# The first layer's in-projection from high and low parts of its operands, with the residual kept in DRAM meanwhile

## The chip, the cores and the metric

The kernel runs on one core of one Trainium2 chip. The metric is the device time of one execution, in microseconds (us), as the median over runs. A core has a matrix engine (TensorE, PE in the rows), a vector engine (VectorE, DVE), a scalar engine (ScalarE, ACT), a general engine (GpSimd, POOL) and SyncE (SP), whose queue issues the weight transfers here. The engines run side by side and meet at semaphores.

## The reference, cut to what matters

Two layers act on 256 context tokens and 256 latent tokens of width 1024. Of the first layer only the input projection is touched:

```python
u_l = rmsnorm(h_l, norm_g[l, 0]) * (1 + sc_a) + sh_a
u_c = rmsnorm(h_c, norm_g[l, 0]) * (1 + csc_a) + csh_a
...
def mixer_ab(u_c, u_l, w_in, w_out, ...):
    p_c = split_cols(u_c @ w_in, AB_SPLITS)
    p_l = split_cols(u_l @ w_in, AB_SPLITS)
    ...
    (q, k, v, output gate | input and forget gates | z, x with B and C, dt)
...
h_l = h_l + g_a * rmsnorm(y_l, norm_g[l, 1])
```

`u` is 512 tokens by 1024, `w_in` is 1024 by 5424 columns: q and k 512 each, v and the output gate o 1024 each, 16 gate columns, z 1024, x (with B and C) 1280, dt 32. After it come an mLSTM and an SSD scan, an output projection, a residual and a mixture of experts; the second layer is of the same size.

## The kernel before, in words

Activations lie transposed in SBUF: feature on the 128 partitions, 512 tokens along the row, so `u` is eight tiles `a_u[:, k, :]` (k = 0 to 7). The residual `h` has the same shape and stays in SBUF for the whole program. The program is a sequence of blocks with a barrier of all engines between them. Weights stream through a ring of three slots of 2 MB (`ring`, pieces of 1024 rows by 512 columns); SP issues piece i once piece i-3 was let go, in a fixed order.

The in-projection is two blocks. `project_gates` makes three small outputs (`pg` 0 to 2: 8, 8 and 32 rows) and then ten tiles of 128 columns of x by 512 tokens. `project_rest` makes 32 such tiles in the order q, k, v (two halves), o (two), z (two), four to a piece. Every tile is eight float32 matmuls (one for each k) into one PSUM bank (`mms`, L358); the trace holds two records for one float32 matmul. The tiles of v have `u` as the stationary operand, all others the weights. Behind each group of four tiles PE also sums one piece of the modulation weights (`row_sums`, L468), and turns a row of those sums (`turn_row`, L475).

In `project_rest` ACT first takes its part in two softplus-like functions (`soft_act`, L713 and L715: an Exp and a Ln, each of which waits for DVE), once for the forget gates and once for dt, and then evicts each tile from PSUM (`pr`, five banks in turn). DVE works out the gate rows (`mlstm_rows`, `ssd_rows`) and then the convolution of ten tiles of x: five operations each (L781 once, L783 four times), with a Silu on ACT (L863) behind each. From the third tile on DVE waits for the Silu of two tiles before. PE needs the rows of DVE once, in `turn_rows`. POOL has nothing to do in this block.

A scheme of high and low parts is already used in two later stages of this kernel, `out_projection` of layer 0 (L1202 to L1214) and `project_rwkv` of layer 1 (L1894 to L1914). There ACT copies an operand into a tile of type float32r (the high part), POOL subtracts that from the weights (the low part, 128x1024 at a time), DVE subtracts it from the activations, and PE adds three products:

```python
def three(wh, wl, xh, xl):
    return [(wh, xh), (wh, xl), (wl, xh)]
```

So a tile of 128x512 over k = 0 to 7 is 24 matmuls of float32r there, one record each, instead of 8 of float32.

## Time and profile before

| | |
|---|---|
| runs | 2682.89, 2684.81, 2694.09 us, median 2684.81 us |
| the profiled execution | 2680.09 us, with a span of 2678.3 us between its first and last instruction |
| granted TensorE clock, mean | 0.895 of full speed |
| PE busy | 2189.2 us, 82% of the span |
| weight loads of PE | 1353.1 us, 51% |
| DVE busy | 988.4 us, 37% |
| ACT busy | 650.2 us, 24% |
| POOL busy | 248.0 us, 9% |

The page also cuts the span into 40 slices of 67 us and gives each engine's busy share in tenths. The two blocks of the in-projection run from 76.7 to 416.3 us, which is the second to the seventh digit. Matmuls are pipelined and their ends are modelled, so starts are the firmer numbers. A number in brackets behind a row is how long the engine had been idle, and for whom.

### The profile page before, as it was taken

The numbers are of one execution on the slowest core, as the hardware profiler recorded it, in microseconds if no ns is written. First come the engines' busy times: TensorE is split into PE (matmuls) and PEld (weight loads), VectorE is DVE, ScalarE is ACT, GpSimd is POOL, SyncE is SP. The second block draws the span as 40 slices with busy tenths as digits, with TensorE's granted clock in tenths as the row PEclk, the third lists the DMA queues.
The fourth block names the chain that finished last, engine by engine and source line by source line (L and its number), as shares of the span: only waits on it lengthen the run. The fifth ranks groups of instructions, "written<-read, shape, count | busy, mean of one in ns | idle before, by whom it ended". The sixth has DMA issues, their size and how long they took to land. (4 is left out here: it accounts for less than half of the span.)

```text
span 2678.3 us, 56972 instructions
## 1 busy us (share of the span) xinstructions
PE 2189.2 (82%) x25395; PEld 1353.1 (51%) x25395; DVE 988.4 (37%) x1594; ACT 650.2 (24%) x1441; POOL 248.0 (9%) x190
## 2 busy tenths in 40 slices
PE   4899999789888897798837869868888889777766
PEld 2344444433375544454423348657887766634333
DVE  0243204666622311111142347556677652311112
ACT  2011213335532200010021232354553420100001
POOL 0000000000043100000010015313131100100000
PEclk8999998888898798899978989979999988797888
DMA  6244431050134459887843013000000023499994
GB/s 212 71 168 153 150 126 63 1 189 0 35 123 160 148 205 326 317 274 263 290 169 111 0 37 105 0 2 4 4 4 4 4 73 118 162 373 349 348 325 159
DMA packets 180666, 376.76 MB, mean 141 GB/s; under 512 B 11210, under 2 KB 40486, under 8 KB 180422
## 3 DMA queue, kind: packets, MB, share of 16 engines
q1 hardware_dynamic: 162830, 339.82, 35.7%
q10 hardware_dynamic: 14136, 20.72, 2.5%
q0 software_dynamic: 3456, 12.58, 1.3%
q8 instruction: 200, 3.28, 0.5%
q14 instruction: 44, 0.36, 0.0%
HBM read 632.36 MB, written 23.86 MB: 245 GB/s over the span
## 5 line engine op out<-in xcount | busy, mean ns | idle before, releaser
L358 PE MATMUL banks<-arena,ring 128*128 128x512 f32 (+3 forms) x1136 | 420.1, 531 | 25.9 <-PEq L305 25.9
L358 PEld LDWEIGHTS banks<-arena,ring 128*128 128x128 f32 (+2 forms) x1136 | 212.3, 188 | 227.9 <-issue 217.0
L1453 PE MATMUL banks<-arena 128*32 128x256 f32 x1696 | 238.0, 430 | 97.4 <-DMA arena<-in_exp_w_up_dram 97.3
L1454 PE MATMUL banks<-arena 128*32 128x256 f32 x1696 | 238.0, 430 | 0.0
L358 PE MATMUL banks<-parts 128*128 128x512 f32 (+1 forms) x1032 | 216.2, 372 | 23.7 <-DVE parts L372 20.5
L358 PEld LDWEIGHTS banks<-parts 128*128 128x128 f32 x1032 | 182.4, 192 | 57.2 <-DVE parts L372 11.5
L1453 PEld LDWEIGHTS banks<-arena 128*32 128x32 f32 x1696 | 107.0, 121 | 189.1 <-DMA arena<-in_exp_w_up_dram 106.1
L2109 PE MATMUL banks<-arena 64*64 64x64 f32 x4224 | 159.9, 225 | 49.2 <-DVE arena L369 18.9
L366 DVE TENSOR_TENSOR arena<-banks,arena 64x256 f32<-64x256 f32 (+3 forms) x128 | 65.2, 511 | 319.2 <-ACT arena L1517 250.2
L2109 PEld LDWEIGHTS banks<-arena 64*64 64x64 f32 x4224 | 148.1, 140 | 53.4 <-DVE arena L369 20.4
L1517 ACT ACTIVATE arena<-banks 64x256 f32<-64x256 f32 x78 | 29.7, 381 | 584.5 <-PE banks L1454 584.5
L2109 PE MATMUL banks<-ring 64*64 64x64 f32 x4224 | 158.7, 224 | 7.2 <-issue 7.0
L358 PE MATMUL banks<-arena 128*64 128x128 f32 (+9 forms) x492 | 132.9, 423 | 36.8 <-PEq L305 25.0
L2109 PEld LDWEIGHTS banks<-ring 64*64 64x64 f32 x4224 | 146.6, 139 | 9.4 <-issue 8.7
L1475 PE MATMUL banks<-arena 128*32 128x256 f32 x1696 | 111.5, 407 | 17.3 <-DMA arena<-in_exp_w_down_dram 17.3
L358 PEld LDWEIGHTS banks<-arena 128*128 128x128 f32 (+5 forms) x492 | 73.3, 194 | 88.8 <-issue 60.0
L1453 PE MATMUL banks<-ring,arena 128*32 128x256 f32 x800 | 102.1, 399 | 8.1 <-DMA ring<-in_exp_w_up_dram 8.0
L1454 PEld LDWEIGHTS banks<-arena 128*32 128x32 f32 x1696 | 106.5, 121 | 0.0
L1214 POOL TENSOR_TENSOR parts<-ring,parts 128x1024 fp32r<-128x1024 f32 x16 | 38.5, 2410 | 711.0 <-ACT parts L1202 711.0
L1454 PE MATMUL banks<-ring,arena 128*32 128x256 f32 x800 | 101.9, 399 | 0.0
L1113 PE MATMUL banks<-arena 128*64 128x256 f32 (+3 forms) x288 | 89.3, 465 | 13.8 <-DVE arena L1146 13.8
L358 PE MATMUL banks<-ring,arena 128*128 128x512 f32 x224 | 98.4, 596 | 1.6 <-DVE arena L366 1.6
(321 smaller groups left out, 3123.2 us busy)
## 6 DMA issues: line engine op xcount, KB each, us to landing
arena<-in_exp_w_gate_dram SPq DMA_DIRECT2D x106, 1024.0 KB
arena<-in_exp_w_up_dram SPq DMA_DIRECT2D x106, 1024.0 KB
arena<-in_exp_w_down_dram SPq DMA_DIRECT2D x53, 2048.0 KB
ring<-in_exp_w_gate_dram SPq DMA_DIRECT2D x50, 1024.0 KB
ring<-in_exp_w_up_dram SPq DMA_DIRECT2D x50, 1024.0 KB
ring<-in_exp_w_down_dram SPq DMA_DIRECT2D x25, 2048.0 KB
ring<-in_w_mod_dram SPq DMA_DIRECT2D x24, 2048.0 KB, 8.3
ring<-in_ab_w_in_dram SPq DMA_DIRECT2D x10, 2048.0 KB, 11.4
```

Source lines behind the costliest of these rows:

```text
L358: m = nc.tensor.matmul(o, a, b, start=first and n == 0, stop=last and n == len(pairs) - 1)
L366: return nc.vector.tensor_tensor(o, a, b, ALU.mult)
L1113: m = nc.tensor.matmul(o[:, c0:c1], a_xt[:, s, hd * SSP:(hd + 1) * SSP], weights_of[it % 3][:, s, c0:c1], start=d == 0 and k == 0, stop=d ...
L1214: nc.gpsimd.tensor_tensor(w_low[:, t % 2], landed(t), whole(w_high[:, t % 2]), ALU.subtract).then_inc(pool_done, pool.tick(("w low", t), * ...
L1453: nc.tensor.matmul(o[r:r + BLOCK, 0:256], x, up[:, k, c], start=k == 0, stop=k == KD - 1)
L1454: m = nc.tensor.matmul(o[64 + r:64 + r + BLOCK, 0:256], x, gate[:, k, c], start=k == 0, stop=k == KD - 1)
L1475: m = nc.tensor.matmul(ps[3 + i % 2][BLOCK * q:BLOCK * q + BLOCK, 0:256], x, w[:, k, 256 * q:256 * q + 256], start=k == 0, stop=k == 3)
L1517: nc.scalar.activation(m_sil[0:64, :], ps[i % 2][64:P, 0:256], ACT.Silu).then_inc(act_done, act.tick(("silu", i)))
L2109: m = nc.tensor.matmul(view(d, n_)[half(d, hf, n_), p, :], now[d][a][rows, p, :], now[d][b][rows, p, :], start=q == 0, stop=q == len(pairs ...
```

## The change

The projection's inputs and weights are split into high and low parts, and each tile is three products over k instead of one. The three small outputs (`pg` 0 to 2) keep float32 operands, `a_u_plain`, which lies where `a_u` lay.

- `u`: ACT writes the high part `u_high` over the room of `h` (`h_parts`), DVE the low part `u_low` in place over `a_u_plain`, from `pg` 2 on, since the three small outputs read `a_u_plain`. For that `h` is stored to DRAM in the block ahead (`save_h`) and loaded again in the block `mlstm` behind.
- weights: for each of 42 jobs (ten in `project_gates`, 32 in `project_rest`) ACT writes a high part and POOL a low part (`split_high`, `split_low`), 128x1024 each, into two rooms in turn; job j may be split once PE is through with job j-2 ("used"). The rooms lie in the later place of z's output, and for the jobs of z in the convolution's room. A weight piece is let go by POOL's last subtraction, and no longer by PE.
- `project_gates` splits jobs 0 to 11, that is its own ten and the first two of the next block. In `project_rest` ACT splits two jobs ahead, in one stream with the evictions.
- v is taken by pieces of 256 rows: a job is two k by 512 columns, times four token tiles, and the four banks are evicted together after the fourth job.
- `row_sums` stands behind the second tile of each group instead of the fourth, `turn_rows` behind job 15 instead of 9, and the Silus of the convolution behind jobs 12 to 21 instead of 8 to 17. `out_projection` and all that follows is as before.

```diff
--- before.py
+++ after.py
-        h = sb("h", [P, KD, T])
+        with nc.sbuf_tensor("h", [P, KD, T], F32) as h:
+            pass
+
+        h_parts = ctx.enter_context(nc.sbuf_tensor("h_parts", [P, KD, T], F32R))
...
+        h_saved = nc.dram_tensor("h_saved", (P, KD, T), F32, kind="Internal").ap()
+        h_saved_done = semaphore("h_saved_done")
...
+        with nc.sbuf_tensor("arena_ahead_of_u", [P, 22608], F32), nc.sbuf_tensor("a_u_plain", [P, KD, T], F32) as a_u_plain:
+            pass
+
+        ctx.enter_context(nc.sbuf_tensor("arena_for_experts", [P, 5120], F32))
+        parts_z = ctx.enter_context(nc.sbuf_tensor("parts_z", [P, 4096], F32R))
+        ctx.enter_context(nc.sbuf_tensor("arena_between", [P, PARTS - 9216], F32))
...
+        split_jobs = [(("x", 2), f) for f in range(2)] + [(key, f) for key in (
+            ("x", 0), ("x", 1), "q", "k", ("v", 0), ("v", 1), ("o", 0), ("o", 1), ("z", 0), ("z", 1)) for f in range(4)]
+        rooms_of_parts = split_rooms()
...
+        def split_high(j):
+
+            i = piece_at[split_jobs[j][0]]
+            act.wait_ge(weights_landed[i % NSLOT], 16 * (i // NSLOT + 1))
+            act.wait_ge(*at(("used", j - 2)))
+            nc.scalar.activation(parts_of(j)[0], landed_part(j), ACT.Copy).then_inc(act_done, act.tick(("w high", j)))
+
+        def split_low(j, *also):
+
+            high, low = parts_of(j)
+            key, f = split_jobs[j]
+            pool.wait_ge(*at(("w high", j)))
+            for label in also:
+                pool.wait_ge(*at(label))
+            last = f == (1 if key == ("x", 2) else 3)
+            nc.gpsimd.tensor_tensor(low, landed_part(j), whole(high), ALU.subtract).then_inc(
+                pool_done, pool.tick(("w low", j), *((let_go(key),) if last else ())))
+
+        N_GATE_JOBS = 10
+        u_low = parts_region(22608 - PARTS, KD, T)
...
+                for j in range(N_GATE_JOBS):
+                    o = bank("pg", 3 + j)
+                    high, low = parts_of(j)
+                    if j == 0:
+                        pe.wait_ge(*at(("u high", KD - 1)))
+                        pe.wait_ge(*at(("w high", 0)))
+                        mms(o, [(high[:, k, :], u_high[:, k, :]) for k in range(KD)], last=False)
+                        pe.wait_ge(*at(("w low", 0)))
+                        mms(o, [(low[:, k, :], u_high[:, k, :]) for k in range(KD)], first=False, last=False)
+                        for k in range(KD):
+                            pe.wait_ge(*at(("u low", k)))
+                            m = mms(o, [(high[:, k, :], u_low[:, k, :])], first=False, last=k == KD - 1)
+                    else:
+                        pe.wait_ge(*at(("w low", j)))
+                        pairs = []
+                        for k in range(KD):
+                            pairs += three(high[:, k, :], low[:, k, :], u_high[:, k, :], u_low[:, k, :])
+                        m = mms(o, pairs)
+                    m.then_inc(pe_done, pe.tick(("pg", 3 + j), ("used", j)))
+
+            def act_():
+                split_high(0)
+                split_high(1)
+                act.wait_ge(h_saved_done, 16)
+                for k in range(KD):
+                    nc.scalar.activation(u_high[:, k, :], a_u_plain[:, k, :], ACT.Copy).then_inc(act_done, act.tick(("u high", k)))
+                for j in range(2, N_GATE_JOBS + 2):
+                    split_high(j)
...
+                    if j == 3:
+                        for k in range(KD):
+                            dve.wait_ge(*at(("u high", k)))
+                            vsub(u_low[:, k, :], a_u_plain[:, k, :], whole(u_high[:, k, :])).then_inc(dve_done, dve.tick(("u low", k)))
...
+                for j in range(N_GATE_JOBS + 2):
+                    split_low(j, *([("pg", 2)] if j == 1 else []))
...
-                    w = weights(key)
-                    if j >= 5:
-                        pe.wait_ge(*at(("pr", "read", j - 5)))
-                    c = slice(f * P, (f + 1) * P)
-                    pairs = [(a_u[:, k, c], w[:, k, :]) if key[0] == "v" else (w[:, k, c], a_u[:, k, :]) for k in range(8)]
-                    mms(ps[j % 5], pairs).then_inc(pe_done, pe.tick(("pr", j), *((let_go(key),) if f == 3 else ())))
-                    if j == 9:
+                    J = N_GATE_JOBS + j
+                    high, low = parts_of(J)
+                    pe.wait_ge(*at(("w low", J)))
+                    if key[0] == "v":
+                        for tt in range(TT):
+                            t = j - f + tt
+                            if f == 0:
+                                pe.wait_ge(*at(("pr", "read", t - 5)))
+                            c, pairs = slice(tt * P, tt * P + P), []
+                            for k in range(2):
+                                pairs += three(u_high[:, 2 * f + k, c], u_low[:, 2 * f + k, c], high[:, k, :], low[:, k, :])
+                            m = mms(ps[t % 5], pairs, f == 0, f == 3)
+                            if f == 3:
+                                m.then_inc(pe_done, pe.tick(("pr", t), *((("used", J),) if tt == TT - 1 else ())))
+                        if f < 3:
+                            m.then_inc(pe_done, pe.tick(("used", J)))
+                    else:
+                        if j >= 5:
+                            pe.wait_ge(*at(("pr", "read", j - 5)))
+                        pairs = []
+                        for k in range(KD):
+                            pairs += three(high[:, k, :], low[:, k, :], u_high[:, k, :], u_low[:, k, :])
+                        mms(ps[j % 5], pairs).then_inc(pe_done, pe.tick(("pr", j), ("used", J)))
+                    if j == 15:
                         turn_rows()
                     m = 4 + j // 4
                     if f == 0 and m > 4:
                         turn_row(0, m - 1, scratch[:], ps[6])
-                    if f == 3:
+                    if f == 1:
...
+                for j, (key, f) in enumerate(jobs):
+                    if j == 22:
+                        act.wait_ge(*at(("conv silu", 9)))
+                    if j + 2 < len(jobs):
+                        split_high(N_GATE_JOBS + j + 2)
+                    if key[0] != "v":
+                        evict(j, key, f)
+                    elif f == 3:
+                        for tt in range(TT):
+                            evict(j - 3 + tt, key, tt)
...
-                    if 8 <= j < 18:
-                        t = j - 8
+                    if 12 <= j < 22:
+                        t = j - 12
...
+            def sp_():
+                sp.wait_ge(h_saved_done, 16)
+                load(nc.sync, h[:], h_saved)
...
+        def save_h():
+
+            nc.sync.dma_start(h_saved, h[:]).then_inc(h_saved_done, 16)
...
-        modulated("u", 0, 0, a_u, 26704)
+        modulated("u", 0, 0, a_u_plain, 26704, sp_=save_h)
```

The order of instructions moves at two places. The first is PE's stream in `project_gates`. Before, behind the three small outputs (8 and 32 rows) the tiles of x follow; `arena` is `a_u`, `ring` the weights:

```order
L358 MATMUL banks<-arena,ring 8x512 [waits weights_landed_1]
L358 MATMUL banks<-arena,ring 8x512 x15
L358 MATMUL banks<-arena,ring 32x512 [waits weights_landed_2]
L358 MATMUL banks<-arena,ring 32x512 x7
L358 MATMUL banks<-arena,ring 128x512 x16
```

Of the change; `h_parts` is `u_high`, `parts_z` holds the weights' two parts, `parts` is `u_low`:

```order
L368 MATMUL banks<-a_u_plain,ring 32x512 [waits weights_landed_2]
L368 MATMUL banks<-a_u_plain,ring 32x512 x7
L368 MATMUL banks<-h_parts,parts_z 128x512 [waits scalar_steps_done]
L368 MATMUL banks<-h_parts,parts_z 128x512 x7
L368 MATMUL banks<-h_parts,parts_z 128x512 [waits gpsimd_steps_done]
L368 MATMUL banks<-h_parts,parts_z 128x512 x7
L368 MATMUL banks<-parts,parts_z 128x512 [waits vector_steps_done] x8
```

The first tile of x now has 24 matmuls in three groups, of which the last eight each wait for DVE's subtraction of one k.

The second place is ACT's stream from the start of `project_rest`. Before, with the second Exp and Ln of `soft_act` ahead of the evictions of q (L847):

```order
L713 ACTIVATE arena<-arena 32x512 [waits vector_steps_done]
L715 ACT_TABLE_LOAD
L715 ACTIVATE arena<-arena 32x512 [waits vector_steps_done]
L847 ACTIVATE arena<-banks 128x512 [waits tensor_steps_done] x4
L480 ACTIVATE scratch<-banks 128x512 [waits tensor_steps_done]
```

Of the change (L793 and L795 are the Exp and the Ln, L680 is `split_high`, L944 the eviction of q, L490 the copy of a modulation row):

```order
L793 ACTIVATE arena<-arena 32x512 [waits vector_steps_done]
L795 ACT_TABLE_LOAD
L795 ACTIVATE arena<-arena 32x512 [waits vector_steps_done]
L680 ACTIVATE parts_z<-ring 128x1024 [waits tensor_steps_done]
L944 ACTIVATE arena<-banks 128x512
L680 ACTIVATE parts_z<-ring 128x1024 [waits tensor_steps_done]
L944 ACTIVATE arena<-banks 128x512
L490 ACTIVATE scratch<-banks 128x512 [waits tensor_steps_done]
```

The splitting for the third tile of q (the first L680 here) stands behind the last Ln on the same engine.

## Rows read from the trace of the kernel before

**Rows 1.** The page, the span in 40 slices: busy tenths of PE and DMA, granted clock
```profile
PE   4899999789888897798837869868888889777766
PEclk8999998888898798899978989979999988797888
DMA  6244431050134459887843013000000023499994
```
**Rows 2.** The timeline of PE from 50 to 440 us: start, duration, instruction
```profile
76.67 91.24 PE L358 MATMUL banks<-arena,ring 128*8 128x512 f32 x208 [11.62 <-PEq L305]
169.50 27.70 PE L358 MATMUL banks<-arena,ring 128*128 128x512 f32 x64 [1.60 <-PEq L305]
197.13 1.92 PE L468 MATMUL banks<-ring,silc 128*32 128x512 f32 x16
...
227.55 1.92 PE L468 MATMUL banks<-ring,silc 128*32 128x512 f32 x16
...
416.29 1.09 PE L919 MATMUL banks<-arena,ident 8*128 8x512 f32 x2 [1.03 <-PEq L305]
```
**Rows 3.** The timeline of DVE from 140 us, and of all engines at 99 us
```profile
99.08 0.68 DVE L665 COPY arena<-banks 32x512 f32<-32x512 f32 x1 [6.19 <-PE banks L358]
...
161.07 0.69 DVE L668 COPY arena<-banks 128x512 f32<-128x512 f32 x1 [6.17 <-PE banks L358]
167.94 0.69 DVE L668 COPY arena<-banks 128x512 f32<-128x512 f32 x1 [6.18 <-PE banks L358]
```
**Rows 4.** The timeline of ACT in out_projection, 740 to 830 us
```profile
739.44 8.41 ACT L1207 ACTIVATE parts<-arena 128x512 fp32r<-128x512 f32 x16
752.97 1.06 ACT L1202 ACTIVATE parts<-ring 128x1024 fp32r<-128x1024 f32 x1 [5.12 <-PE banks L358]
...
823.69 1.06 ACT L1202 ACTIVATE parts<-ring 128x1024 fp32r<-128x1024 f32 x1 [4.38 <-PE banks L358]
```
**Rows 5.** The tile parts: duration ns min/median/max, first and last start
```profile
L1894 POOL TENSOR_TENSOR parts<-ring,parts x27: 2343/2395/2795, 1582.0 to 1714.7; 128x1024 fp32r<-128x1024 f32 x27
L372 DVE TENSOR_TENSOR parts<-arena,parts x24: 676/677/2834, 740.1 to 1590.6; 128x512 fp32r<-128x512 f32 x24
```
**Rows 6.** The timeline of PE in out_projection
```profile
745.66 88.87 PE L358 MATMUL banks<-parts 128*128 128x512 f32 x384 [9.19 <-DVE parts L372]
```
**Rows 7.** The timeline of ACT from 140 us: start of project_rest
```profile
169.47 1.28 ACT L713 ACT_TABLE_LOAD   x1 [93.16 <-PEq L305]
...
193.48 0.63 ACT L715 ACTIVATE arena<-arena 32x512 f32<-32x512 f32 x1
```
**Rows 8.** The timeline of DVE: first tile of the convolution
```profile
204.26 0.55 DVE L781 TENSOR_SCALAR arena<-arena,vec 128x512 f32<-128x512 f32 x1
204.84 3.11 DVE L783 SCALAR_TENSOR_TENSOR arena<-arena,vec 128x512 f32<-128x512 f32 x4
```
**Rows 9.** The timeline of all engines in project_rwkv
```profile
1627.71 2.40 POOL L1894 TENSOR_TENSOR parts<-ring,parts 128x1024 fp32r<-128x1024 f32 x1 [3.97 <-ACT parts L1902]
1628.22 2.44 DVE L369 TENSOR_TENSOR arena<-arena 128x512 f32<-128x512 f32 x1 [2.75 <-ACT arena L1914]
```
**Rows 10.** The timeline of ACT: eviction of o and a Silu
```profile
298.94 0.60 ACT L853 ACTIVATE arena<-banks 128x512 f32<-128x512 f32 x1 [4.62 <-PE banks L358]
299.56 1.28 ACT L863 ACT_TABLE_LOAD   x1
300.85 0.63 ACT L863 ACTIVATE arena<-arena 128x512 f32<-128x512 f32 x1
```
**Rows 11.** The DMA issues: line, count, KB, median us to landing
```profile
ring<-in_w_mod_dram SPq DMA_DIRECT2D x24, 2048.0 KB, 8.3
ring<-in_ab_w_in_dram SPq DMA_DIRECT2D x10, 2048.0 KB, 11.4
```
**Rows 12.** Two stretches: busy us (count) PE, PEld, DVE, ACT, POOL; clock, DMA share, GB/s
```profile
60.00:70.00 10.00, 5.05 (x11) 1.49 (x10) 4.06 (x3) 4.86 (x8) 0.00 (x0) 0.99 0.00 0
...
736.00:760.00 24.00, 14.81 (x59) 12.16 (x59) 13.47 (x19) 12.44 (x20) 7.93 (x4) 0.73 0.55 175
```

## What the change should do to the time, foretold before it was run

> **What bounds the kernel now.** I read the page first. PE is near 9 tenths in the second to the seventh slice and its clock there is near full [rows 1]; these slices are the in-projection. The timeline of PE says how tightly: records of the projection follow each other from 76.67 us, with one gap of 1.6 us at 169.5, up to the first instruction of the next block at 416.29 [rows 2]. Nobody is waited for inside, so this stretch is as long as PE's own work, and a shorter tile shortens the program one for one, as long as whoever feeds PE keeps up. DVE's evictions in project_gates give the period of a float32 tile: 167.94 - 161.07 = 6.87 us [rows 3]. The rest block lasts 416.29 - 169.50 = 246.8 us; 32 tiles are 219.8 of it, and 27.0 are all else: eight row sums of 1.9 us [rows 2], the turned rows, the hand-over.
>
> **What a tile costs in three products.** The same form is in the trace: out_projection makes 24 products of 128x512 per weight room, and ACT begins its next split when PE is through with a room. From 752.97 to 823.69 there are 13 such periods, 70.72 / 13 = 5.44 us [rows 4], that is 0.227 us a product. 42 tiles would save 42 x (6.87 - 5.44) = 60.1 us if PE never waited. The feeders per job are one ACT copy, 1.06 us [rows 4], and one POOL subtraction, 2.4 us, at most 2.8 [rows 5]. From the end of tile j to the low part of tile j+2 that is about 3.7 us with a tenth for each of two semaphores, and tile j+1 covers 5.44. In steady state they are hidden with 1.7 us to spare; without that cover each pair of tiles would lose what the chain has over 5.44.
>
> What is left is where the cover is missing.
>
> **project_gates.** The three small outputs stay; `pg` 2 is evicted at 99.08 [rows 3]. By then ACT has made the first two weight parts and u_high (eight copies at 8.41 / 16 = 0.53 us each [rows 4]), from 76.7 to about 83. The store of h is issued when the block ahead starts, before 60 us; no transfer ran from 60 to 70 us there [rows 12], and a weight piece of 2 MB lands in 8.3 to 11.4 us [rows 11], so it has landed by 75, against a need at 79. I cost it at nothing; the cover is the small outputs, and it costs only if it lands after 95. PE can do 16 of the first 24 products at once (3.6 us, to 102.7). The last eight wait for DVE's subtractions, which DVE begins behind the eviction, at 99.8. POOL's subtraction of job 1 is released by the same `pg` 2 and starts first. Beside such an operation a DVE addition took 2.44 us, started at 1628.22 and over 0.55 us after POOL's end [rows 9], and the longest u-type subtraction took 2.83, where the median is 0.68 [rows 5]. So the first of the eight ends near 102.2 and the last near 107.1; tile 0 ends at 107.4, 2.9 us late. (Without the collision it would be 105.5.) Nine more tiles: 107.4 + 49.0 = 156.4.
>
> **The hand-over.** Job 11 is split in this block and may only start when tile 9 is done: 0.1 + 1.06 + 0.1 + 2.4, and POOL must end before the barrier. Then the barrier as before, from DVE's end at 167.94 + 0.69 = 168.63 to 169.50 [rows 2, 3], 0.9. PE starts the next block at 161.0 and not at 158: 3.0 us more of gap than before.
>
> **project_rest, its start.** This is the largest loss. Jobs 10 and 11 are ready, and job 12 is split by ACT behind the second Ln. In the trace of before ACT ends that Ln at 194.11, in a block that began for it at 169.47: 24.6 us [rows 7], most of it waiting for DVE's gate rows. Before this cost nothing, since PE had tiles that needed only a free bank. Now job 12 is ready at 24.6 + 1.1 + 0.1 + 2.4 + 0.1 = 28.3 us, while PE has work for 2 x 5.44 + 1.9 (row sums) = 12.8. PE stands for 15.5 us. POOL has nothing to do until then, so DVE's rows take no longer. Behind a wait PE comes back at a lower clock: out_projection began at 745.66 after 9.19 us idle [rows 6], was through with its first room at 752.97, 7.3 us and not 5.44, and the stretch shows 0.73 of the full clock [rows 12]. That is 1.9 us once; the same loss at the hand-over, if it comes, ends within the stall.
>
> **project_rest, the remainder.** 30 tiles are 163.2 us. Of the 27.0 us of other work 1.9 lie ahead of the stall, and about 0.7 at the end fall away, since the last row sums now have two tiles behind them: 24.4. The four evictions of v (0.6 each behind a split of 1.06) make the next token tile wait once, 0.5. End: 28.3 + 163.2 + 24.4 + 1.9 + 0.5 = 218.3 us after 161.0, that is 379.3 against 416.3.
>
> **The sum**: 60.1 saved, 23.1 given back, **37.0 us** less. Everything behind is as before; reloading h, 2 MB, lies in `mlstm`, in whose two slices, the seventh and eighth, the DMA engines are busy for 1 tenth and none [rows 1]; I cost it at nothing, and it would cost only if that block were shorter than the 11 us of a landing [rows 11]. The profiled execution took 2680.1, so 2643.1; it lies 4.7 below the median of the runs (2684.8), from which the same saving gives 2647.8. I take 2646. What a measurement of this kernel can tell from no change is about 0.5%, 13.4 us.
>
> **The convolution** has to be weighed too. DVE's five operations on a tile take 0.55 + 3.11 and with gaps 3.7 us [rows 8]; each reads SBUF, and POOL now holds it off for 2.4 us in each tile's period. A period is 5.44 and with its share of row sums 6.2 us, which leaves 3.8. It just fits, with almost two periods between the release of a convolution and the Silu that needs it. If nothing collided it would cost 0; if every tile met POOL twice, 3.7 + 2 x 2.4 = 8.5 us against 6.2, over eight tiles 18 us, of which the slack takes some 5. I take 0 and keep 13 for the range. The Trainium skill ("SBUF — State Buffer", Who interferes with whom) says that a VectorE instruction with two SBUF inputs and a GpSimd one that reads SBUF exclude each other for the whole instruction. The trace agrees (2.44 us against 0.68), and by that rule the convolution is no freer than I put it.
>
> **ACT's tables.** Behind tiles 16 to 21 the Sigmoid of o and the Silu of the convolution alternate, so each needs two table loads, where before two tiles had that. The trace has an eviction at 298.94, the load at 299.56 for 1.28 us, and the Silu at 300.85 right behind it [rows 10]. ACT's work in such a period is 1.06 + 0.60 + 0.63 + 2 x 1.28 = 4.9 us, under 5.44. "ScalarE: Activation LUTs" (the Trainium skill, What ACT_TABLE_LOAD costs) adds a drain, and puts a switch at 2.66 us; the trace shows no such gap, and with that figure the period would be an estimated 7.6 us and the result that of the second rival below.
>
> **The rivals.**
> - Convolution late, as above: DVE paces tiles 14 to 21, saving near 24, **2657 to 2660**. For it: DVE has 0.1 us of spare in a period. Against it: the two periods of slack. 12 in 100.
> - ACT paces the tiles of o. If each switch held ACT for twice the row's 1.28 us, six periods would be 7.4 us each, 2.0 over 5.44, less the spare of 1.7 and the row sums: about 7 us, **2653**. Against it: the row. 3 in 100.
> - Weights late. The piece for the next group is let go about 3.7 us behind a group's second tile and is needed five tiles later, 21 us, two pieces at once. At 8.3 to 11.4 us each [rows 11] they fit even one behind the other; 5 us late in a few groups gives **2656**. 4 in 100.
> - The stall is shorter than I think, because something lets job 12 go early: **2630**. Nothing in ACT's order speaks for it. 3 in 100.
> - Slower: the chain from the end of a tile to the low part of the next but one is longer than a tile. Then the period is (chain + 5.44) / 2. The 37 us are gone when it is 1.23 us longer over 30 tiles, that is with a chain of 7.9 us instead of 3.7, and by 8.8 us the kernel is slower by 0.5%, **2698** and up. POOL's subtraction would have to take 7 us beside DVE's work; in 27 executions beside DVE none passed 2.8 [rows 5]. 2 in 100.
> - The change doesn't do what it says: products on these operands run no faster than those of float32, 6.87 a tile, and only the losses stay, 2680 + 23 = **2703**. The period of out_projection [rows 4] is against it. 1 in 100.
>
> My forecast, a saving of 30 to 43, has the remaining 75. The range of 8 in 10 goes from 2632 (a stall some 10 us shorter) to 2661 (the late convolution). Faster by over 0.5% (below 2671): 0.94. Within: 0.03. Slower: 0.03.
>
> **What would show it.** In the timeline of PE: tiles of 24 records 5.44 us apart; a wait for `parts` of DVE in the first tile of x; a gap near 5 us before the rest block; a gap of 15 us behind two tiles and one row sum, released by POOL's L690, whose own wait is for ACT L680; clock below 1.0 in the two stretches behind the gaps; the next block's first matmul near 379. Wrong would be a gap before each tile released by POOL (the chain), by ACT behind L971 (convolution or tables), or by a transfer (weights). Nothing past 379 should be shorter or longer by more than a few us.

## The result, and the profile after

The changed kernel takes 2657.46 us (median of 4 runs, 2651.06 to 2659.08) where the one before takes 2687.21 beside it: a ratio of 0.9891 (95% interval 0.9859 to 0.9922). A second set of 6 runs of it gave 2650.86 us (2646.89 to 2656.08) against 2686.93: 0.9868 [0.9837, 0.9899]. Both medians lie in the predicted range of 2632 to 2661, 11 and 5 us above the predicted 2646. As a saving that is 29.8 us in the first set, at the lower edge of the 30 to 43 that were forecast, and 36.1 in the second. The profiled execution took 2651.06 us with a span of 2649.3, where the sum had given 2643.1.

The page, the same three rows as in [rows 1] (PE's busy tenths, the granted clock, DMA):

```profile
PE   5879999788796987797838869867887888877776
PEclk7989998778897999998968889979999988888788
DMA  7244540320324478987731012000000023599994
```

The timeline of PE, to be laid beside [rows 2]. Line numbers have moved: L368 here is L358 there, L478 is L468, L1031 is L919.

```profile
75.42 22.52 PE L368 MATMUL banks<-a_u_plain,ring 128*8 128x512 f32 x48 [11.61 <-PEq L315]
97.86 4.00 PE L368 MATMUL banks<-h_parts,parts_z 128*128 128x512 f32 x16
101.70 4.53 PE L368 MATMUL banks<-parts,parts_z 128*128 128x512 f32 x8
...
160.10 0.47 PE L368 MATMUL banks<-h_parts,parts_z 128*128 128x512 f32 x1 [3.95 <-PEq L315]
...
172.93 1.92 PE L478 MATMUL banks<-ring,silc 128*32 128x512 f32 x16
188.14 0.80 PE L368 MATMUL banks<-h_parts,parts_z 128*128 128x512 f32 x1 [13.29 <-POOL parts_z L690]
...
380.48 1.09 PE L1031 MATMUL banks<-arena,ident 8*128 8x512 f32 x2 [1.04 <-PEq L315]
```

PE, which had one gap of 1.60 us before, now has two large ones: 3.95 us at the hand-over and 13.29 us behind two tiles and a row sum. The projection lasts from 75.42 to 380.48, 305.06 us, where it was 416.29 - 76.67 = 339.62: 34.6 us less. The whole execution is 29.0 less (2680.09 - 2651.06). The remainder is elsewhere: the projection begins 1.25 us earlier, and what follows it is 6.8 us longer (2649.3 - 380.48 = 2268.8 against 2678.3 - 416.29 = 2262.0). The last experiments deal with that.

The stretches of the projection (busy us with counts of PE, PEld, DVE, ACT, POOL; then the granted clock, DMA share, GB/s):

```profile
75.42:160.10 84.68, 80.09 (x288) 49.66 (x289) 15.99 (x21) 16.77 (x21) 30.13 (x15) 0.98 0.36 123
...
160.10:188.10 28.00, 14.75 (x64) 10.46 (x64) 25.43 (x32) 12.39 (x16) 2.36 (x2) 0.76 0.42 173
188.10:196.00 7.90, 7.86 (x27) 6.37 (x28) 7.62 (x9) 0.35 (x1) 2.77 (x1) 0.78 0.50 164
196.00:280.00 84.00, 83.75 (x411) 64.25 (x410) 27.38 (x28) 26.01 (x36) 34.04 (x14) 1.00 0.51 185
280.00:380.48 100.48, 99.44 (x482) 76.54 (x481) 25.35 (x32) 48.20 (x56) 35.26 (x15) 1.00 0.46 164
```

The second row is the stall: PE is busy for 14.75 of 28.00 us, DVE for 25.43 of them, and the clock is at 0.76. The third is the restart: PE is busy throughout, at a granted clock of 0.78, so about 7.9 x 0.22 = 1.7 us are lost. From 196 on the clock is full and up to the barrier at the end PE is out of work for 0.25 us only, behind the first half of v. The splits of weights and what holds that of the third tile of the block (job 12), in the timelines of ACT and of POOL:

```profile
111.82 1.06 ACT L680 ACTIVATE parts_z<-ring 128x1024 fp32r<-128x1024 f32 x1 [4.43 <-PE banks L368]
...
156.19 1.06 ACT L680 ACTIVATE parts_z<-ring 128x1024 fp32r<-128x1024 f32 x1 [4.42 <-PE banks L368]
...
184.09 0.63 ACT L795 ACTIVATE arena<-arena 32x512 f32<-32x512 f32 x1
184.62 1.04 ACT L680 ACTIVATE parts_z<-ring 128x1024 fp32r<-128x1024 f32 x1
```
```profile
185.74 5.13 POOL L690 TENSOR_TENSOR parts_z<-ring,parts_z 128x1024 fp32r<-128x1024 f32 x2 [26.08 <-ACT parts_z L680]
```

The split (L680) of job 12 starts right behind the last Ln of the dt rows (L795), and POOL had stood for 26 us waiting for it. Ready at 188.14, that is 28.0 us into the block. Elsewhere splits follow PE's tiles: from 111.82 to 156.19 there are eight periods, 5.546 us each.

The changed kernel was profiled a second time, in the second set of runs (2651.25 us). A stretch of 305 us again and a median 28 to 30 us below the kernel before had been expected of it; the stretch took 307.17 us (the first block 86.03, the second 221.14), and the median is 36.1 us below. In the timeline of ACT the splits behind the first and the second tile of x:

```profile
109.37 1.06 ACT L680 ACTIVATE parts_z<-ring 128x1024 fp32r<-128x1024 f32 x1 [24.59 <-PE banks L368]
116.39 1.06 ACT L680 ACTIVATE parts_z<-ring 128x1024 fp32r<-128x1024 f32 x1 [5.96 <-PE banks L368]
```

The second tile took 7.0 us there and not 5.5. PE had waited for DVE in the last eight products of the tile ahead, and the granted clock from 109.08 to 116.30 was 0.76, where it was 1.00 over the same tile in the first profile. The restart behind the stall also cost more, 2.4 us. So the length of the stretch moves by 2 us between executions of the same kernel; of the six profiles that have this first tile with all its products and its waits, two show a second tile of 7 us.

### The profile page after: what moved, and what is told of

It reads as the page before. It is cut to its first block and busy times, and to the rows that moved or that the text cites. A ratio compares the mean times of both kernels' runs of the same rounds, so it can differ in the third digit from the quotient of the medians.

```text
span 2649.3 us, 57779 instructions
## 1 busy us (share of the span) xinstructions
PE 2141.1 (81%) x25731; PEld 1417.6 (54%) x25731; DVE 1010.6 (38%) x1602; ACT 706.4 (27%) x1499; POOL 350.6 (13%) x232
## 5 line engine op out<-in xcount | busy, mean ns | idle before, releaser
L368 PE MATMUL banks<-parts 128*128 128x512 f32 (+1 forms) x1096 | 241.0, 373 | 23.6 <-DVE parts L382 20.4
L368 PEld LDWEIGHTS banks<-parts 128*128 128x128 f32 x1096 | 194.3, 192 | 59.7 <-DVE parts L382 11.5
L368 PE MATMUL banks<-arena,ring 128*128 128x256 f32 (+2 forms) x544 | 161.7, 460 | 12.7 <-PEq L315 12.7
L368 PE MATMUL banks<-arena 128*64 128x128 f32 (+9 forms) x492 | 135.8, 430 | 36.8 <-PEq L315 25.0
L2225 PEld LDWEIGHTS banks<-ring 64*64 64x64 f32 x4224 | 143.3, 135 | 12.7 <-issue 12.2
L368 PE MATMUL banks<-h_parts,parts_z 128*128 128x512 f32 x416 | 133.9, 402 | 17.2 <-POOL parts_z L690 13.3
L368 PEld LDWEIGHTS banks<-arena,ring 128*128 128x128 f32 (+1 forms) x544 | 105.4, 195 | 67.1 <-issue 56.0
L368 PEld LDWEIGHTS banks<-arena 128*128 128x128 f32 (+5 forms) x492 | 74.3, 196 | 89.5 <-issue 60.5
L1784 POOL DMA_INDIRECT arena<-y_sorted,slot_ids x12 | 11.3, 945 | 746.1 <-DMA y_sorted<-arena 743.1
L1569 PE MATMUL banks<-ring,arena 128*32 128x256 f32 x800 | 99.9, 393 | 8.9 <-DMA ring<-in_exp_w_up_dram 8.9
L690 POOL TENSOR_TENSOR parts_z<-ring,parts_z 128x1024 fp32r<-128x1024 f32 x34 | 84.3, 2482 | 158.4 <-ACT parts_z L680 139.1
```

Of the source, the lines that this page charges most:

```text
L368: m = nc.tensor.matmul(o, a, b, start=first and n == 0, stop=last and n == len(pairs) - 1)
L690: nc.gpsimd.tensor_tensor(low, landed_part(j), whole(high), ALU.subtract).then_inc(pool_done, pool.tick(("w low", j), *((let_go(key),) if ...
L1569: nc.tensor.matmul(o[r:r + BLOCK, 0:256], x, up[:, k, c], start=k == 0, stop=k == KD - 1)
L1784: nc.gpsimd.indirect_dma_start(m_yg[:, t, a, :], None, y_sorted, bass.IndirectOffsetOnAxis(ap=slots[:, t, a:a + 1], axis=0)).then_inc(y_ga ...
L2225: m = nc.tensor.matmul(view(d, n_)[half(d, hf, n_), p, :], now[d][a][rows, p, :], now[d][b][rows, p, :], start=q == 0, stop=q == len(pairs ...
```

## The experiments

A single run is one execution: its total says little, and its profile is what is read. Three times named below are read off the timeline of PE in the same way everywhere: *gates* is project_gates, from its first matmul to the first of project_rest (84.68 us in the changed kernel), *rest* is from there to the first matmul of `mlstm` (220.38), and the stretch is their sum (305.06). Their counterparts before are 92.83, 246.79 and 339.62.

### The splits between the gate rows

The two exponentials of `em` and the dt rows are no longer ahead of the tiles in ACT's order: jobs 12 and 13 are split behind the first rows, job 14 behind `em`, the dt rows follow.

```diff
+                for j in range(2):
+                    one_job(j, *jobs[j])
                 for e in range(2):
...
+                one_job(2, *jobs[2])
                 soft_act(tmp32, "dt")
-                for j, (key, f) in enumerate(jobs):
+                for j in range(3, len(jobs)):
```

> ACT's stream at the start of project_rest is put in another order: splits and evictions of the first two tiles of q stand behind the first Ln, those of the third ahead of the second Exp. All work is done. Theory (the stall of 13 to 15 us behind two tiles comes from the place of the split in ACT's stream): the gap goes; the lower clock behind the hand-over, hidden until now, costs 1.9 us in its place, DVE's rows become a few us longer beside POOL, and the block of 220.4 us becomes 205 to 208. Rival (DVE's gate rows bind, wherever the splits stand): the gap only moves, and the block stays above 217. Against the kernel before: 40 to 45 us less in all, a ratio near 0.984.

Measured: 2642.44 us (4 runs), ratio 0.9833 [0.9817, 0.9849]. Rest 208.14 us, just over the 205 to 208 expected and 12.2 less than in the changed kernel, gates 84.55. PE's gap of 13.29 has become one of 2.42, behind another wait, in the timeline of ACT:

```profile
184.16 0.63 ACT L973 ACTIVATE arena<-arena 8x512 f32<-8x512 f32 x1 [7.72 <-DVE arena L841]
...
185.87 1.04 ACT L680 ACTIVATE parts_z<-ring 128x1024 fp32r<-128x1024 f32 x1
```

ACT waits 7.7 us for DVE's rows at `em`, and the split of the fifth tile of the block stands behind it. So the order on ACT was the cause of the stall: only the order was changed, and 11 of its 13 us went. DVE's rows themselves were slower here, because POOL works beside them now; in the timeline of DVE one addition takes 2.78 us

```profile
170.04 2.78 DVE L379 TENSOR_TENSOR arena<-arena 8x512 f32<-8x512 f32 x1
```

while POOL's subtraction runs from 169.55 to 172.28. In the changed kernel, where POOL stands idle, the same row takes 0.68 us.

### Saving and reloading h, alone

The kernel before, with nothing added but the two transfers of h.

```diff
+            def sp_():
+                sp.wait_ge(h_saved_done, 16)
+                load(nc.sync, h[:], h_saved)
...
-            block(pe_, act_, dve_)
+            block(pe_, act_, dve_, None, sp_)
...
-        modulated("u", 0, 0, a_u, 26704)
+        modulated("u", 0, 0, a_u, 26704, sp_=save_h)
```

> The kernel before with one part of the change alone: h is stored to DRAM in the block ahead of the projection and loaded again in mlstm; the projection stays in float32. Theory (it is hidden): the projection's 339.6 us and mlstm's 112.3 us stay within 1 us, ratio 1.000. Rival (the reload is what made mlstm 2.8 us longer after the change): mlstm has 115 us here too.

Measured: 2685.65 us (10 runs), ratio 0.9987 [0.9964, 1.0011]; gates 92.72, rest 246.79, stretch 339.51 against 339.62. The round trip costs nothing that can be measured, and the projection does not feel it. `mlstm`, with the reload in it, took 114.82 us, and not the 112.3 that were expected to stay within 1 us; that is the rival's 115, and the last experiment takes it up.

### Two products instead of three

One product in three is left out, that of the stationary operand's low part with the high part of the moving one: the weights' low part, and in the tiles of v that of `u`. So the projection is less exact than the reference asks for; the splitting, the waits and the transfers stay.

```diff
-                            pairs += three(high[:, k, :], low[:, k, :], u_high[:, k, :], u_low[:, k, :])
+                            pairs += three(high[:, k, :], low[:, k, :], u_high[:, k, :], u_low[:, k, :])[:2]
```

> The changed kernel with the third product of each k left out (low stationary part times high moving part) in the in-projection, so 16 products a tile and a less exact result; all splits are made as before. It asks how much of the chain ACT, POOL, DVE is covered. Theory: a tile is 3.7 us, about as long as the chain of 3.6 us; the ten tiles of project_gates take 3.7 to 3.8 us each; in project_rest the stall grows by 3.7 us to 17, and in the tiles of o, where ACT needs 4.9 us and DVE's convolution 6.1 beside POOL, the period is near 6 us and no longer 5.5. The stretch from the first matmul of project_gates to mlstm, 305.1 us, becomes 240 to 248. Rival (ACT alone sets the pace of o, DVE is not held off by POOL): 4.9 us in those tiles, 5 us less in all. Rival (feeders far from binding): 3.7 us throughout, the stretch 232.

Measured: 2592.36 us (4 runs), ratio 0.964 [0.9624, 0.9656]; stretch 241.87 (240 to 248 expected), gates 70.23. In the timeline of ACT the first two and the last of nine splits, then in that of PEld (weight loads) two waits:

```profile
112.65 1.06 ACT L680 ACTIVATE parts_z<-ring 128x1024 fp32r<-128x1024 f32 x1 [3.95 <-PE banks L368]
116.36 1.06 ACT L680 ACTIVATE parts_z<-ring 128x1024 fp32r<-128x1024 f32 x1 [2.64 <-PE banks L368]
...
143.14 1.06 ACT L680 ACTIVATE parts_z<-ring 128x1024 fp32r<-128x1024 f32 x1 [2.72 <-PE banks L368]
```
```profile
116.24 0.19 PEld L368 LDWEIGHTS banks<-h_parts,parts_z 128*128 128x128 f32 x1 [0.37 <-POOL parts_z L690]
119.95 0.19 PEld L368 LDWEIGHTS banks<-h_parts,parts_z 128*128 128x128 f32 x1 [0.18 <-POOL parts_z L690]
```

A tile is (143.14 - 112.65) / 8 = 3.81 us. Here the weight load of each tile waits 0.2 to 0.4 us for POOL: from the split at 116.36 to the weight load at 119.95 it is 3.6 us, with a semaphore ahead of it the 3.7 of the prediction. That chain is as long as a tile of 16 products, so it shows at last. Under tiles of 24 it is hidden with 1.8 us to spare, and there PE's own work, the products, sets the time of the changed kernel. The stall is 16.97 us, as expected.

The six tiles of o are another matter. Their period was expected near 6 us, or 4.9 if ACT alone set it:

```profile
265.32 0.64 ACT L970 ACTIVATE arena<-arena 128x512 f32<-128x512 f32 x1 [0.94 <-DVE arena L862]
265.86 1.04 ACT L680 ACTIVATE parts_z<-ring 128x1024 fp32r<-128x1024 f32 x1
```

From 249.61 to 277.42 there are five periods, 5.56 us each, with ACT never waiting for PE but once for 0.19, and for DVE's convolution (L862) up to 0.94. So where the tables alternate, ACT and DVE together need as long as a tile of 24 products: the changed kernel has next to nothing to spare there.

### The rooms of the parts elsewhere

Tiles took 5.49 to 5.55 us and not 5.44. The parts of the gates' jobs are put where those of z lie, and nothing else is changed.

```diff
-            high, low = rooms_of_parts[key[0] == "z"][j % 2]
+            high, low = rooms_of_parts[key[0] == "z" or j < 10][j % 2]
```

> The weight parts of the ten jobs of project_gates lie in the convolution's room (the one that z's jobs use) and not in z's output; nothing else. It tests why a tile takes 5.54 us in this block where out_projection has 5.44 and the jobs of z 5.48. Theory (it hangs on where the operands lie in SBUF): 5.48 here, the block 84.7 us becomes 84.1. Rival (it is DVE's evictions, transfers or the block's own waits): 5.54 stays.

Measured in a single run: 2648.96 us; gates 84.18, rest 220.60. Splits in the timeline of ACT:

```profile
112.60 1.06 ACT L680 ACTIVATE parts<-ring 128x1024 fp32r<-128x1024 f32 x1 [4.36 <-PE banks L368]
...
156.55 1.06 ACT L680 ACTIVATE parts_z<-ring 128x1024 fp32r<-128x1024 f32 x1 [4.38 <-PE banks L368]
```

The period is (156.55 - 112.60) / 8 = 5.494, where the same eight in the changed kernel give (156.19 - 111.82) / 8 = 5.546. The old place gives 5.546 to 5.548 in the three other profiles of the same eight periods (the first edit, the second profile of the changed kernel, the later reload), so the difference is no scatter: the place of the operands does set about 0.05 us of a tile, 2 ns a product. Gates became 0.5 us shorter. That is too little to be seen in the kernel's time, and what it is about the place is not shown.

### A gentler hand-over

From here on edits are added to the version with the splits between the rows. Job 11 is split at the start of project_rest instead of at the end of project_gates.

```diff
-                for j in range(2, N_GATE_JOBS + 2):
+                for j in range(2, N_GATE_JOBS + 1):
...
+                split_high(N_GATE_JOBS + 1)
```

> e1 with the split of job 11 moved over the barrier: ACT's and POOL's part for it are the first of project_rest. Theory: the gap of 3.95 us between the two blocks becomes 1.6 and the lower clock behind it goes, so project_gates is 2.3 us shorter; but DVE's rows now meet one more subtraction and begin half a us later, so ACT's exponentials and with them the split of job 14 come some 3 us later, and project_rest grows from 208.1 to 210 or 211: nothing gained in the sum. Rival (the rows have slack enough): project_rest stays at 208 or falls to 206, and the gain of 2.3 stays.

Measured in a single run: 2638.99 us; gates 82.35, rest 212.29, stretch 294.64 against 292.69 with the first edit alone: no net gain, as expected, but a loss of 2 us, since rest had been put at 210 to 211. In the timeline of PE:

```profile
161.86 0.47 PE L368 MATMUL banks<-h_parts,parts_z 128*128 128x512 f32 x1 [1.12 <-PEq L315]
...
192.61 0.79 PE L368 MATMUL banks<-h_parts,parts_z 128*128 128x512 f32 x1 [6.26 <-POOL parts_z L690]
```

The gap at the barrier falls from 3.95 to 1.12 (1.6 was expected): 2.8 us were the split of job 11. They come back at the next wait, 6.26 us where it was 2.42. That wait ends on DVE's rows, and these became later: POOL's subtraction of job 11 now runs beside the first of them, which takes 2.91 us (0.68 in the changed kernel), and ACT's exponentials of `em` start 25.4 us into the block instead of 23.1. The longer gap also brings the lower clock back: from 175 to 200 it is 0.86, where the first edit alone had 1.00.

### The low part early

POOL's subtraction of job 1 no longer waits for `pg` 2, so it does not start together with DVE's eight subtractions. A memset behind `pg` 2 lets the weight piece go in its place.

```diff
-            last = f == (1 if key == ("x", 2) else 3)
+            last = f == 3
...
-                    split_low(j, *([("pg", 2)] if j == 1 else []))
+                    split_low(j)
+                    if j == 1:
+                        pool.wait_ge(*at(("pg", 2)))
+                        nc.gpsimd.memset(slot_gate[:, 0:1], 0.0).then_inc(pool_done, pool.tick(let_go(("x", 2))))
```

> e5 with POOL's subtraction of job 1 freed from its wait for the third small output (a one-element memset behind that output lets the weight piece go instead), so that it runs at 80 us and no longer beside DVE's first subtraction of u. Theory (that collision cost 1.9 us): DVE's eight subtractions take 5.6 us and not 7.1, and the first tile of x ends 1.5 to 1.9 us sooner; project_rest as in e5. Rival (the eight are slow for another reason): no change.

Measured in a single run: 2637.55 us; gates 79.46, 2.9 less, rest 212.99 (212.29 before this edit). The collision in the changed kernel (all engines):

```profile
98.09 2.84 POOL L690 TENSOR_TENSOR parts_z<-ring,parts_z 128x1024 fp32r<-128x1024 f32 x1 [19.21 <-PE banks L368]
98.58 7.10 DVE L382 TENSOR_TENSOR parts<-a_u_plain,h_parts 128x512 fp32r<-128x512 f32 x8
...
102.12 0.19 PEld L368 LDWEIGHTS banks<-parts,parts_z 128*128 128x128 f32 x1 [0.41 <-DVE parts L382]
```

POOL runs from 98.09 to 100.93. DVE's eight subtractions, begun at 98.58, take 7.10 us; the later ones are 0.60 us each (0.19 of weight load and 0.41 of wait), so the first was through only 2.9 us after it began, and PE waits for each of the next. With the collision gone DVE's eight take 4.88 us, and the first tile's last eight products wait for nobody (the rows of the next experiment show the same). From its first product to the first of the second tile it is 6.00 us instead of 8.21, a gain of 2.2 where 1.5 to 1.9 had been expected. The other 0.7 us of the 2.9 are no gain: the small outputs ran at a lower clock in the profile of the version before (0.90 from 80 to 100 us, here 1.00).

### All together

Besides these, jobs 12 to 16 are split and the first five tiles evicted ahead of `em` and the dt rows, and the gates' parts lie in the room of z's.

```diff
-                for j in range(2):
+                for j in range(5):
                     one_job(j, *jobs[j])
```

> e6, the rooms of e4 for project_gates, and ACT's order changed further: the first five jobs of project_rest are split and evicted ahead of the exponentials of m and of the second soft_act, which wait for DVE. Theory (DVE's rows are not needed before the convolution, so nothing has to wait for them here): no gap behind the first tiles, project_gates 80 us and project_rest 203 to 205, the stretch 284 against 305.1 of the change and 339.6 before; about 2632 in the median, a ratio near 0.979. Rival (DVE's rows, now beside five subtractions, delay the convolution, and it paces the tiles of o): project_rest stays near 208, with ACT waiting for DVE behind tiles 14 to 21.

Measured: 2628.02 us (6 runs, 2622.03 to 2642.08), ratio 0.9794 [0.976, 0.9829]; gates 79.06, rest 203.88, stretch 282.94 (284 expected), which is 22 us less than in the changed kernel and 57 less than before. In the timeline of PE no gap over 0.25 us is left between the hand-over and the last turned row:

```profile
98.99 3.99 PE L368 MATMUL banks<-h_parts,parts 128*128 128x512 f32 x16
102.81 2.32 PE L368 MATMUL banks<-parts 128*128 128x512 f32 x8
104.97 0.39 PE L368 MATMUL banks<-h_parts,parts 128*128 128x512 f32 x1
...
357.61 0.95 PE L485 MATMUL banks<-quarter_sum,scratch 128*128 128x2 f32 x8
359.60 1.77 PE L1040 MATMUL banks<-arena,ident 8*128 8x512 f32 x2 [1.04 <-PEq L315]
```

Rest is 9.1 us less than in the version before: the gap of 6.3, and most of the remainder the restart behind it. All 6 runs are below all 6 of the changed kernel beside them (2646.89 to 2656.08), 22.8 us in the medians. With the losses taken away that the prediction had listed, 56.7 of the 60.1 us are had that it gave for the products alone.

### Is mlstm longer, and for the reload?

`mlstm` took 115.02 us after and 112.26 before, 2.8 of the 6.8 us that are lost behind the projection. It holds the reload of h. The kernel before with the round trip alone had 114.82, but one value of a block that may scatter decides nothing. Two versions reload `h` later, behind mlstm_out, and the kernel before ran twice more.

```diff
-            block(pe_, act_, dve_, None, sp_)
+            block(pe_, act_, dve_)
...
         def ssd_prepare():
...
-            block(pe_, act_, dve_)
+            def sp_():
+                sp.wait_ge(h_saved_done, 16)
+                load(nc.sync, h[:], h_saved)
+
+            block(pe_, act_, dve_, None, sp_)
```

> The kernel before once more, for the scatter of the blocks behind the in-projection. In its first profiled execution mlstm lasted 112.3 us (528.55 - 416.29); in the kernels that reload h inside mlstm it lasted 112.6 to 118.4, most about 115.5. Theory A, the reload lengthens mlstm by some 3 us: this run shows 112 to 113. Theory B, scatter between executions alone: this run may show anything from 112 to 118.

> The kernel before a third time. Theory A: mlstm 112 to 113 us again. Theory B: 112 to 118, so that its three values spread as those with the reload do.

> The changed kernel, but h is reloaded in the block behind mlstm_out (ssd_prepare) instead of in mlstm. Theory A (the reload of 2 MB costs mlstm some 3 us): mlstm 112 to 113 us, total about 2648 instead of 2651. Theory B (scatter): mlstm 112 to 118 and a total of 2647 to 2656, as the changed kernel had it.

> The version with all edits (splits between the rows, gentler hand-over, early low part, other rooms), with h reloaded in ssd_prepare. Theory A: mlstm 112 to 113 us where it was 116.5, total near 2619 to 2624. Theory B: mlstm 112 to 118, total 2622 to 2630.

Single runs: before again 2675.34 and 2687.69 us with `mlstm` at 112.26 and 114.55; the later reload 2652.3 with 115.96; all edits with the later reload 2630.66 with 116.60, where the same edits with the reload in `mlstm` had 116.50. The two totals, 2652.3 and 2630.66, are no shorter than scatter alone was expected to leave them (2647 to 2656, and 2622 to 2630). The longest two without a reload in it are longer than the changed kernel's own 115.02. So theory A falls: the reload is not what lengthens the block. Its stretch in five executions, among them the shortest and the longest (columns as above): before a second and a third time, the rooms elsewhere, the low part early, and all with the reload later. One fence for each:

```profile
415.76:528.02 112.26, 94.83 (x280) 51.94 (x280) 72.93 (x92) 33.26 (x85) 0.00 (x0) 0.86 0.08 28
```
```profile
417.94:532.49 114.55, 98.08 (x280) 52.51 (x280) 73.18 (x92) 33.21 (x86) 0.00 (x0) 0.83 0.07 27
```
```profile
381.06:493.67 112.61, 94.79 (x280) 51.26 (x280) 73.09 (x92) 33.27 (x86) 0.00 (x0) 0.86 0.06 23
```
```profile
368.22:486.59 118.37, 101.40 (x280) 53.84 (x280) 73.01 (x92) 33.22 (x86) 0.00 (x0) 0.81 0.06 21
```
```profile
357.66:474.26 116.60, 99.56 (x280) 53.00 (x280) 73.00 (x92) 33.26 (x85) 0.00 (x0) 0.82 0.01 4
```

The same 280 matmuls take 94.8 us of PE where the granted clock is 0.86 and 101.4 where it is 0.81, and DVE's and ACT's times do not move. The block's length follows the clock that it is given, with the reload (112.61 and 118.37) and without it (112.26 and 116.60).

What sets that clock is open. The four profiles with the projection in float32 (before three times, the round trip alone) have 112.26 to 114.82 us; of the ten with split operands eight have 115.02 or more. That speaks for a part of the 2.8 us being a consequence of the denser projection, a rival that no run here isolates. The later reload has a price of its own: ssd_prepare took 555.24 - 540.91 = 14.3 us there, and 583.85 - 573.06 = 10.8 in the third profile of the kernel before; PE stands for 4.29 us at its end, where it is 0.86 in the changed kernel, so this block is shorter than the landing and waits for it. `mlstm` is the better place for it.

## Why the prediction was right

**The tiles.** Foretold 5.44 us a tile and 60.1 us in all; by the starts of PE's products a tile is 5.55 us in x, q, k and o, 5.49 in z, and a job of v 5.60 or 5.49. Over the 9 and the 30 tiles of the sum this is 3.8 us more than 5.44 each. It is the term that was mis-sized: it was taken from a projection whose parts lie elsewhere, and the run with other rooms moved it by half of the difference. That the period is mostly PE's own work is shown by the run with two products: 336 fewer of them at 0.23 us are 77 us, of which the stretch lost 63; the rest is the longer stall (3.7) and the feeders, which come to light once the tile is shorter.

**The first tile of x.** Foretold 30.7 us behind the block's start (107.4 - 76.67), 2.9 late; measured 106.07 - 75.42 = 30.65. With the collision taken away it was 28.3 (104.97 - 76.66), 2.3 less, where the working had 1.9 for it (107.4 - 105.5). The sum has no term for a lower clock behind this tile's waits: in the first profile it cost nothing, in the second 1.5 us.

**The hand-over.** Foretold 3.0 us more of gap; measured 3.95, 2.35 more than the 1.60 of [rows 2], and 1.12 with the split taken away.

**The stall.** Foretold: job 12 ready at 28.3 us and PE standing for 15.5. Measured 28.04, with 13.29 of idle; the rest of the difference is that PE's tiles ahead of it ran at the lower clock behind the hand-over, which costs nothing there, as was said. The order on ACT is shown to be its cause by the first experiment, which had 11 of the 13 us back.

**The restart.** Foretold 1.9, measured about 1.7 in the first profile and 2.4 in the second.

**v, the convolution and the tables.** The timeline of ACT shows the four evictions of v, and later an alternation of the tables; that of DVE shows a tile of the convolution and the start of the next:

```profile
251.40 1.06 ACT L680 ACTIVATE parts_z<-ring 128x1024 fp32r<-128x1024 f32 x1 [4.37 <-PE banks L368]
252.36 2.04 ACT L948 ACTIVATE arena<-banks 128x512 f32<-128x512 f32 x4
257.49 1.06 ACT L680 ACTIVATE parts_z<-ring 128x1024 fp32r<-128x1024 f32 x1 [3.09 <-PE banks L368]
...
299.29 1.28 ACT L950 ACT_TABLE_LOAD   x1
300.59 0.60 ACT L950 ACTIVATE arena<-banks 128x512 f32<-128x512 f32 x1
301.20 1.28 ACT L971 ACT_TABLE_LOAD   x1
302.50 0.63 ACT L971 ACTIVATE arena<-arena 128x512 f32<-128x512 f32 x1
303.69 1.06 ACT L680 ACTIVATE parts_z<-ring 128x1024 fp32r<-128x1024 f32 x1 [0.56 <-PE banks L368]
```
```profile
289.12 0.55 DVE L861 TENSOR_SCALAR arena<-arena,vec 128x512 f32<-128x512 f32 x1 [4.79 <-ACT arena L971]
289.71 5.13 DVE L863 SCALAR_TENSOR_TENSOR arena<-arena,vec 128x512 f32<-128x512 f32 x4
296.06 0.55 DVE L861 TENSOR_SCALAR arena<-arena,vec 128x512 f32<-128x512 f32 x1 [1.23 <-ACT arena L971]
```

The period with v's evictions is 257.49 - 251.40 = 6.09, about 0.5 over a tile of 5.5 to 5.6, as foretold. Of the ten tiles of the convolution five took 5.13 to 5.34 us for their last four steps, where they took 3.11 [rows 8], that is about one meeting with POOL each and not the feared two; the other five took 3.11. DVE waits for ACT, 1.23 to 4.79 us, ahead of each tile from the fourth to the ninth, so this lies in slack and the cost is 0, as taken. ACT had 0.56 us of idle left in its tightest period, ahead of 303.69, with two table loads of 1.28 us in it and the next instruction right behind each. The rule in "ScalarE: Activation LUTs" (the Trainium skill, What ACT_TABLE_LOAD costs) would have put 2.66 us to each switch; here, too, the measurement says 1.28 and no drain that can be seen.

**What the sum missed.** By these terms the stretch should have been 302.6 (84.3 + 218.3) and was 305.06. The tiles are 3.8 us over; the hand-over (0.6), the readiness of job 12 (0.3) and the restart (0.2) came out shorter than foretold and hide a part of it, so the 2.5 are closer than the terms deserve. In the second profile the stretch is 4.6 over. The other 5.5 us between 2643.1 and the profiled 2651.06 lie outside the stretch, where "everything behind is as before" held for the instructions and not for the clock: the same 280 matmuls of `mlstm` alone move by 6 us between executions. `attention` took 63.8 us before and 67.9 after, with 0.95 and 0.87 of the clock, and `rwkv_chunks` became 4.0 us shorter (424.8 and 420.8), with 0.95 and 0.96. So "nothing past 379 should be shorter or longer by more than a few us" just about held, but its ground, unchanged instructions, is not enough: blocks moved by 4 us either way, and their clocks moved with them. For blocks other than `mlstm` this is argued from one profile on each side, not tested. No run tells whether the denser projection lowers the clock that `mlstm` gets: with it `mlstm` had 0.81 to 0.86, without it 0.83 to 0.86.

**What was luck.** The mechanism came out as told, wait by wait. The number in the first set of runs, 2657.46, lies 11 us above the forecast and at the 2657 to 2660 of the late convolution, which the rows rule out; it is inside the range because that had been stretched to 2661 for this rival, and not because the scatter of the clock had been allowed for.

## What to carry to other kernels

When an engine gets a new task that feeds the bound engine, read the whole queue of that engine at the start of the block: here a copy of 1 us stood behind 25 us of waiting that had been harmless for as long as nobody needed ACT, and it took 13 of the 60 us that the faster products gave. A gain just ahead of such a wait is given back at it; here only a better order took it away. And price the period of a pipelined unit from the same form at the same place, and leave a margin for the clock: here the sum was 2.5 and 4.6 us off in the stretch in two profiles of one kernel, and 8 us in the whole.

## What was not expected of the hardware

- The spacing of float32r products of one form depends on where their operands lie in SBUF: 5.546 us for 24 in one pair of rooms, 5.494 in another, 0.9% of a tile. The edit changed nothing but the room. In v, where `u` is the stationary operand, the first two jobs of each half take 5.60 us and the last two 5.49, in the same two rooms; these differ in the part of `u` that they read.
- The same block of 280 matmuls was granted a clock between 0.81 and 0.86 in 14 profiled executions of eleven kernels, and took from 118.4 to 112.3 us by it. A difference of 3 us in one block between two profiles shows nothing unless the clock beside it is the same.
- A DVE addition of 8x512 elements (0.68 us alone) took 2.78 us beside POOL's subtraction, and ended 0.54 us after it. That was at 170.04 in the version with the splits between the rows; at 175.27 there a scan of 8x256 (0.68 alone) took 2.76 and ended 0.54 after POOL too; the 128x512 addition of [rows 9] took 2.44 and ended 0.55 after. So what the meeting costs is what is left of the other engine's instruction, not a share of DVE's own size.
